# Seams of a two-layer hybrid block: the second statistic from sums of x*z, DMAs that accumulate into x, and a new order of VectorE's work

## The chip, the cores and the metric

One core of one Trainium2 chip runs the whole program. The metric is the device time in microseconds of one execution. In the texts PE is TensorE, DVE is VectorE, ACT is ScalarE, POOL is GpSimd and SP is SyncE. Lower is better.

## The reference

Two layers over 512 latent tokens and 256 context tokens (768 together, width 1024). Every sub-layer has the same frame, and the change is about that frame:

```python
def _pre(x, g, mod, k):
    return _rmsnorm(x, g) * (1.0 + mod[:, 3 * k + 1][:, None]) + mod[:, 3 * k][:, None]

def _post(x, y, g, mod, k, weight):
    return x + weight * mod[:, 3 * k + 2][:, None] * _rmsnorm(y, g)
# _rmsnorm: y = xf * rsqrt(mean(xf * xf) + EPS), times g
# per layer: x = _post(x, swiglu(_pre(x, .., 0)), ..); x = _post(x, mixer(_pre(x, .., 1)), ..)
#            x = _post(x, swiglu(_pre(x, .., 2)), ..)      the mixer: S5 heads beside 2-D Fourier heads
```

So between two sub-layers stand two root-mean-square statistics per token: that of the output y, and that of the new x.

## The kernel before, in words

Activations lie with the 1024 features in 8 chunks (KC) of 128 partitions and the 768 tokens along the free axis; the context takes columns 0 to 255. xT is the residual stream, yT the output of a stage. Weights come in units of 128x1024 values: SP loads one to `raw` (3 slots), ScalarE makes a rounded high part wH (L458), VectorE the rest wL (L465), and each product is three matmuls: high by high, high by low, low by high (L473). The activations are split in the same way into hH and hL. The counters w_hi, w_lo and w_used order this; `late` names a stage's one unit whose split waits for the end of the stage before: the third unit of the next stage.

The plan has six stages: f10, m0, f20 (layer 0: feed-forward, mixer, feed-forward), then f11, m1, f21 (layer 1; f21 has only the latent tokens, and so has the seam before it). Between two stages lies a seam. In the kernel before it goes like this.

- `last_chunks` (TensorE) makes the eight output chunks of a stage in three PSUM slots; `last_adds` (VectorE, L992, L1006, L1010) adds them to yT; ScalarE squares yT (L1384, L1398, L1401), GpSimd adds the squares of chunks 0 to 5 up in sumY (L1265), and TensorE sums over features with a matmul against ones (L1302), 32 columns to a block, so that VectorE can flip a row of sums into columns (L1310).
- ScalarE's root, VectorE's reciprocal (L1462), and a matmul with the identity (L1317) spread 1/rms over all partitions in PSUM.
- VectorE scales the eight chunks of y by it and by coefP, called P (L1471); the scaled output is weight*gate*norm(y). GpSimd adds chunks 0 to 3 into xT and VectorE chunks 4 to 7 (both L1282). VectorE then makes the low part of the late unit.
- ScalarE squares the new x (L1411), TensorE sums, and flip, root, reciprocal (L1487) and spread follow a second time.
- `pre_vector`: per chunk VectorE scales x into tmpN (L1496), ScalarE adds the shift and rounds to hH (L1423), VectorE makes hL (L1500). TensorE's `first_groups` takes the chunks as they come, with 2 units (mixer, f10) or 3 (feed-forward) held in PSUM at once, the last three chunks unit by unit.
- `keep_clock` (L1326) is filler on TensorE: products of the identity that nobody reads. `head_weights` makes products for the Fourier heads, copied to CW by ScalarE at the start of the mixer.

In the f1 stages and the mixers x is spilled to memory and its space reused; GpSimd reloads it before the end. In a mixer, `mix_tensor` goes on with projections (`proj`), between which it makes the inputs of the S5 states for a quarter of the heads (`state_inputs`); VectorE then turns, scans (L2105, L2106) and turns back each quarter. The first scan stands behind the low part of unit 7 in VectorE's order, and so behind projection 4. Each engine runs its instructions in the written order; semaphores are the only order between engines.

## Time and profile before

| | us |
|---|---|
| median of 3 runs | 2648.77 (2648.14 to 2652.62) |
| the profiled execution | 2646.27 |
| its span | 2644.5 |
| PE busy | 2586.2 (98%) |
| DVE busy | 1596.0 (60%) |
| POOL busy | 816.1 (31%) |
| ACT busy | 714.7 (27%) |

The span is the time between the first and the last instruction of the profile; outside it lie 1.8 us. A busy PE is not a useful PE: at the seams it runs sums and filler. Times in the rows below count from the start of the span.

### The profile page before, as it was taken

The numbers are of one execution on the slowest core, as the hardware profiler recorded it, in microseconds if no ns is written. First come the engines' busy times: TensorE is split into PE (matmuls) and PEld (weight loads), VectorE is DVE, ScalarE is ACT, GpSimd is POOL, SyncE is SP. The second block draws the span as 40 slices with busy tenths as digits, with TensorE's granted clock in tenths as the row PEclk, the third lists the DMA queues.
The fourth block names the chain that finished last, engine by engine and source line by source line (L and its number), as shares of the span: only waits on it lengthen the run. The fifth ranks groups of instructions, "written<-read, shape, count | busy, mean of one in ns | idle before, by whom it ended". The sixth has DMA issues, their size and how long they took to land.

```text
span 2644.5 us, 40750 instructions
## 1 busy us (share of the span) xinstructions
PE 2586.2 (98%) x17044; PEld 2429.9 (92%) x17044; DVE 1596.0 (60%) x2238; ACT 714.7 (27%) x1050; POOL 816.1 (31%) x1286
## 2 busy tenths in 40 slices
PE   6999999999999999999999999999999999999998
PEld 5999999998989899999999899999999878888886
DVE  6688878766574676676676633433343684544443
ACT  4222212123334411212113412122122424322223
POOL 1278876832140100000001148667651131000001
PEclk9999999999999999999999999999999999999999
DMA  9534444453364234434432422222223565233331
GB/s 338 154 123 156 157 143 133 161 187 132 117 194 144 79 98 136 130 108 138 136 104 91 109 67 83 94 92 90 94 88 116 189 196 163 72 96 96 96 96 64
DMA packets 346831, 334.54 MB, mean 127 GB/s; under 512 B 52496, under 2 KB 319896, under 8 KB 343576
## 3 DMA queue, kind: packets, MB, share of 16 engines
q1 hardware_dynamic: 284344, 198.19, 25.7%
q10 hardware_dynamic: 52288, 77.20, 8.7%
q0 software_dynamic: 10016, 56.56, 5.6%
q8 instruction: 134, 2.20, 0.3%
q14 instruction: 49, 0.40, 0.0%
HBM read 287.40 MB, written 44.50 MB: 126 GB/s over the span
## 4 chain that ended last, share of the span: by engine, by line
PE 86%; DVE 8%; POOL 2%; issue 1%; ACT 1%; DMA 1%; SPq 0%; DVEq 0%; POOLq 0%; ACTq 0%
PE ps L473 81%; POOL xT L1282 1%; DVE tmpN L1496 1%; DVE hL L1500 1%; PE ps L1302 1%; PE ps L1317 1%; DVE zb L2105 1%; DVE zd L2106 1%; PE ps L1050 1%; ACT wH L458 1%; PE ps L1069 1%; DVE zc L2118 0%; PE ps L1326 0%; DVE SR L2122 0%; PE ps L1702 0%
## 5 line engine op out<-in xcount | busy, mean ns | idle before, releaser
L473 PE MATMUL ps<-hH,wH 128*128 128x384 f32 (+1 forms) x2928 | 1013.5, 346 | 8.5 <-DVE hL L1500 8.0
L473 PE MATMUL ps<-hH,wL 128*128 128x384 f32 (+1 forms) x2928 | 1004.9, 343 | 0.0
L473 PE MATMUL ps<-hL,wH 128*128 128x384 f32 (+1 forms) x2928 | 1004.5, 343 | 0.0
L465 DVE TENSOR_TENSOR wL<-raw,wH 128x1024 fp32r<-128x1024 f32 x300 | 396.4, 1332 | 493.2 <-ACT wH L458 491.7
L473 PEld LDWEIGHTS ps<-hH,wH 128*128 128x128 f32 x2928 | 549.9, 188 | 35.4 <-DVE hL L1500 7.4
L473 PEld LDWEIGHTS ps<-hH,wL 128*128 128x128 f32 x2928 | 550.1, 188 | 18.1
L473 PEld LDWEIGHTS ps<-hL,wH 128*128 128x128 f32 x2928 | 550.2, 188 | 17.8
L473 PE MATMUL ps<-midH,wH 128*128 128x384 f32 (+1 forms) x1232 | 424.0, 344 | 2.9 <-DVE yT L948 2.5
L473 PE MATMUL ps<-midH,wL 128*128 128x384 f32 (+1 forms) x1232 | 421.5, 342 | 0.0
L473 PE MATMUL ps<-midL,wH 128*128 128x384 f32 (+1 forms) x1232 | 421.3, 342 | 0.0
L458 ACT ACTIVATE wH<-raw 128x1024 fp32r<-128x1024 f32 x300 | 310.9, 1049 | 366.2 <-PE ps L473 349.5
L1265 POOL TENSOR_TENSOR sumY<-sq 128x768 f32<-128x768 f32 (+1 forms) x6 | 10.0, 1659 | 1039.7 <-ACT sq L1384 1039.7
L584 DVE SCALAR_TENSOR_TENSOR adaW<-adaW,siluC 128x384 f32<-128x384 f32 x520 | 329.0, 684 | 0.8
L926 DVE TENSOR_TENSOR midF<-ps,sgate 128x768 f32<-128x768 f32 (+1 forms) x88 | 78.4, 890 | 318.1 <-PE ps L473 317.9
L948 DVE TENSOR_TENSOR yT<-ps,yT 128x768 f32<-128x768 f32 (+1 forms) x256 | 223.2, 885 | 71.3 <-PE ps L473 71.3
L473 PEld LDWEIGHTS ps<-midH,wH 128*128 128x128 f32 x1232 | 231.3, 188 | 13.4 <-DVE yT L948 5.3
L473 PEld LDWEIGHTS ps<-midL,wH 128*128 128x128 f32 x1232 | 231.4, 188 | 6.8
L473 PEld LDWEIGHTS ps<-midH,wL 128*128 128x128 f32 x1232 | 231.3, 188 | 6.8
L882 ACT ACTIVATE midH<-midF 128x768 fp32r<-128x768 f32 (+1 forms) x88 | 69.8, 793 | 575.0 <-DVE midF L926 575.0
L875 ACT ACTIVATE sgate<-ps 128x768 f32<-128x768 f32 (+1 forms) x88 | 66.9, 760 | 216.7 <-PE ps L473 206.1
L930 DVE TENSOR_TENSOR midL<-midF,midH 128x768 fp32r<-128x768 f32 (+1 forms) x88 | 81.8, 930 | 0.0
L666 ACT ACTIVATE modraw<-ps 128x3 f32<-128x3 f32 x76 | 9.1, 172 | 240.7 <-PE ps L473 240.7
(284 smaller groups left out, 2261.3 us busy)
## 6 DMA issues: line engine op xcount, KB each, us to landing
raw<-in_ffn_gu_dram SPq DMA_DIRECT2D x176, 512.0 KB, 3.9
adaW<-in_w_ada_dram ACTq DMA_DIRECT2D x40, 1536.0 KB, 7.0
raw<-in_ffn_down_dram SPq DMA_DIRECT2D x88, 512.0 KB, 3.5
x_d<-xT POOLq DMA_DIRECT2D x4, 3072.0 KB, 11.2
xT<-x_d POOLq DMA_DIRECT2D x4, 3072.0 KB, 10.6
ada_early<-in_w_ada_dram POOLq DMA_DIRECT2D x6, 1536.0 KB, 18.7
W_d<-gW POOLq DMA_DIRECT2D x16, 512.0 KB, 3.8
VT_d<-gVT ACTq DMA_DIRECT2D x16, 512.0 KB, 3.0
```

Source lines behind the costliest of these rows:

```text
L458: nc.scalar.activation(wH[:, n % SPLIT_SLOTS, :], raw[:, n % RAW_SLOTS, :], ACT.Copy).then_inc(w_hi, 1)
L465: nc.vector.tensor_tensor(wL[:, n % SPLIT_SLOTS, :], raw[:, n % RAW_SLOTS, :], wH[:, n % SPLIT_SLOTS, :].bitcast(f32), ALU.subtract).then_ ...
L473: ins = nc.tensor.matmul(dst, a, b, start=first and n == 0, stop=last and n == 3 * len(pairs) - 1)
L584: ins = stt(at, w[:, k], siluC[:, k, v:v + 1], adaP[:] if i == 3 else at, ALU.mult, ALU.add)
L875: nc.scalar.activation(sb_pair(sgate[:, f % 2, :], F.tok0), ps_pair(tile_slot(F, g), F.tok0), ACT.Silu)\
L882: nc.scalar.activation(midH[:, f % 4, F.tok0:TOK], midF[:, f % 2, F.tok0:TOK], ACT.Copy).then_inc(mid_hi, 1)
L926: nc.vector.tensor_tensor(sb_pair(midF[:, f % 2, :], F.tok0), ps_pair(tile_slot(F, g), F.tok0), sb_pair(sgate[:, f % 2, :], F.tok0), ALU.m ...
L930: nc.vector.tensor_tensor(midL[:, f % 4, F.tok0:TOK], midF[:, f % 2, F.tok0:TOK], midH[:, f % 4, F.tok0:TOK].bitcast(f32), ALU.subtract).t ...
L948: ins = nc.vector.tensor_tensor(sb_pair(yT[:, m, :], F.tok0), ps_pair(tile_slot(F, g + m), F.tok0), sb_pair(yT[:, m, :], F.tok0), ALU.add)
L1050: ins = nc.tensor.transpose(ps[:, 6 + a, t * 128:(t + 1) * 128], gV[:, a, t, :], ident[:])
L1069: ins = nc.tensor.matmul(ps[32 * p:32 * p + 32, 6 + g2, c0:c1], Bw[half, a, dd, p, :], rhs(half, a, dd, p), start=first, stop=last)
L1282: engine.tensor_tensor(xT[:, m, N.tok0:TOK], xT[:, m, N.tok0:TOK], yT[:, m, N.tok0:TOK], ALU.add)\
```

## The change

For each chunk, as it comes in the tail of a stage, VectorE also makes x*P*y (`cross_z`, P the factor that y will be scaled by but for 1/rms; z is P*y/rms(y)) and adds up those of chunks 0 to 5. TensorE sums the squares of y with weights of 1 and of P^2 at once (statP, columns 1 and 2) in bank 7, five chunks between the last chunks of the stage, and sums the cross products in bank 6 behind the stage. The sum of squares of the new x then is the old one (sumX is kept) plus 2*sum(x*P*y)/rms(y) plus sum(P^2*y^2)/rms(y)^2, made by VectorE in `new_sums` on six columns. GpSimd no longer adds squares or chunks of x: it makes the low part of the late unit (`late_lo`) and issues, for chunks 1 to 7, a DMA each that accumulates yT into xT; VectorE adds chunk 0. The row of 1/rms(y) is copied from PSUM to SBUF (rowY). VectorE scales y two chunks ahead (three in the latent seam) of making hL, within one loop (`joined_chunk`). `first_groups` waits for each unit by itself, interleaves all eight chunks, and holds three units in the mixer too, so the projections between which the state inputs stand begin at 3. Some of the mixer's loads move behind the fourth and eighth chunk. x has to be back before the tail instead of before its scaling. The last stage's end keeps the old way.

```diff
-    def first_groups(pe, base, count, pre, between=None):
-
-        pe.wait_ge(w_lo, base + count)
-        lead = KC - 3
+    def first_groups(pe, base, count, pre, between=None, cw_ready=None):
+
+        lead = KC if pre.after else KC - 3
         order = [(k, u) for k in range(lead) for u in range(count)]
         order += [(k, u) for u in range(count) for k in range(lead, KC)]
         for k, u in order:
             if u == 0:
                 pe.wait_ge(h_lo, KC * pre.nth + k + 1)
+            if k == 0:
+                pe.wait_ge(w_lo, base + u + 1)
+                if u == 1 and cw_ready:
+                    pe.wait_ge(cw, cw_ready)
+                if u == 2:
+                    pe.wait_ge(row_y, pre.after.nth + 1)
...
+    def cross_sums(pe, S, m):
+
+        pe.wait_ge(cross_x, cross_count(S, m))
+        return row_sums(pe, 6, crossed(S, m), S.tok0, TOK, m == 0, m == KC - 1)
+
+    def square_sums(pe, S, m, t0, t1, first=False, last=False):
+
+        return row_sums(pe, 7, sq[:, m, :], t0, t1, first, last, statP[:, m, :])
...
+            while S.next and m >= 2 and summed < m:
+                pe.wait_ge(sq_y, KC * S.post.nth + summed + 1)
+                square_sums(pe, S, summed, S.tok0, TOK, summed == 0)
+                summed += 1
...
+            wait_back(dve, S.post)
+            dlink(dve, nc.vector.memset(statP[:], 1.0))
+            dsync(dve)
+            dlink(dve, nc.vector.tensor_tensor(statP[:, :, 1:3], coefP[:], coefP[:], ALU.mult))
...
+            if S.next:
+                dve.wait_ge(S.read, S.read0 + m + 1)
+                ins = cross_z(dve, S, m, token_segments(S.tok0))
+                if 0 < m < CROSS_SUMMED:
+                    dlink(dve, ins)
+                    dsync(dve)
+                    ins = nc.vector.tensor_tensor(crossed(S, 0)[:, S.tok0:TOK], crossed(S, 0)[:, S.tok0:TOK],
+                                                  crossed(S, m)[:, S.tok0:TOK], ALU.add)
+                if m < CROSS_SUMMED - 1:
+                    dlink(dve, ins)
+                else:
+                    ins.then_inc(cross_x, 1)
...
+    def late_lo(pool, n):
+
+        if n >= NU:
+            return
+        pool.wait_ge(w_hi, n + 1)
+        nc.gpsimd.tensor_tensor(wL[:, n % SPLIT_SLOTS, :], raw[:, n % RAW_SLOTS, :],
+                                wH[:, n % SPLIT_SLOTS, :].bitcast(f32), ALU.subtract).then_inc(w_lo, 1)
+
+    def post_pool(pool, N, S):
+        for n in S.late:
+            late_lo(pool, n)
         wait_back(pool, N)
-        for m in POOL_CHUNKS:
...
+        for m in range(1, KC):
             pool.wait_ge(y_norm, KC * N.nth + m + 1)
-            add_to_x(pool, nc.gpsimd, N, m, x_new_pool)
-
-    def row_sums(pe, bank, squares, t0, t1, first, last):
+            pool.dma_start(xT[:, m, N.tok0:TOK], yT[:, m, N.tok0:TOK], accum_op=ALU.add).then_inc(x_added[m - 1], 16)
...
+    def post_tensor(pe, N, S):
+        if S.next is None:
+            end_sums(pe, N, S)
+            return
+        nxt = S.next
+        pe.wait_ge(sq_y, KC * N.nth + KC - 2)
+        square_sums(pe, S, KC - 3, N.tok0, TOK)
+        if N.tok0 == 0:
+            for m in (KC - 2, KC - 1):
+                pe.wait_ge(sq_half, 2 * N.nth + m - (KC - 2) + 1)
+                square_sums(pe, S, m, 0, HALF)
+        for m in (KC - 2, KC - 1):
+            pe.wait_ge(sq_y, KC * N.nth + m + 1)
+            ins = square_sums(pe, S, m, N.tok0 or HALF, TOK, False, m == KC - 1)
+        ins.then_inc(ss_y, 1)
+        for m in (0, KC - 2, KC - 1):
+            ins = cross_sums(pe, S, m)
+        ins.then_inc(ss_x, 1)
+        pe.wait_ge(rs_y, N.nth + 1)
+        spread_matmuls(pe, 4, 5, N.tok0, rstd, bc_y, bc_y_ctx)
+        keep_clock(pe, 2)
+        pre_spread(pe, nxt)
         if S.tag.startswith("f1"):
             head_weights(pe, S.gen)
-        else:
-            keep_clock(pe, 10)
-        wait_x(pe, N, 0)
         keep_clock(pe, 3)
+        pe.wait_ge(h_tmp, KC * nxt.nth + 1)
+        keep_clock(pe, 2)
+        pe.wait_ge(h_hi, KC * nxt.nth + 1)
...
+    def cross_z(dve, S, m, segments):
+
+        for t0, t1, v in segments:
+            ins = nc.vector.scalar_tensor_tensor(crossed(S, m)[:, t0:t1], yT[:, m, t0:t1], coefP[:, m, v:v + 1],
+                                                 xT[:, m, t0:t1], ALU.mult, ALU.mult)
+        return ins
...
+        if S.next:
+            root(act, rstdX[:], sumX[:], N.tok0, sum_x, N.nth + 1, sd_x)
+            act.wait_ge(y_norm, KC * N.nth + 1)
+            for t0, t1, v in token_segments(N.tok0):
+                ins = nc.scalar.activation(rowY[:, t0:t1], seg_ps(4, 5, v), ACT.Copy)
+            ins.then_inc(row_y, 1)
...
+    def scale_part(N, m, t0, t1, v, row):
+        return nc.vector.scalar_tensor_tensor(yT[:, m, t0:t1], yT[:, m, t0:t1], coefP[:, m, v:v + 1], row,
+                                              ALU.mult, ALU.mult)
+
+    def scale_y(dve, N, m):
+        for t0, t1, v in token_segments(N.tok0):
+            ins = scale_part(N, m, t0, t1, v, rowY[:, t0:t1] if N.has_next else seg_ps(2, 3, v))
+        ins.then_inc(y_norm, 1)
+
+    def add_part(t0, t1):
+        return nc.vector.tensor_tensor(xT[:, 0, t0:t1], xT[:, 0, t0:t1], yT[:, 0, t0:t1], ALU.add)
+
+    def new_sums(dve, N, S):
+
+        b = N.tok0 // 128
+        r, d, c, x = (t[:, b:6] for t in (rstd, sumD, cross, sumX))
+        dve.wait_ge(rs_y, N.nth + 1)
+        for b0, b1, v in [(b, 2, CTXV), (2, 6, LAT)][b // 2:]:
+            dlink(dve, nc.vector.tensor_tensor(sumD[:, b0:b1], turnedY[:, b0:b1, 1 + v], rstd[:, b0:b1], ALU.mult))
+        dsync(dve)
+        dlink(dve, nc.vector.tensor_tensor(d, d, r, ALU.mult))
+        dsync(dve)
+        dlink(dve, nc.vector.tensor_tensor(x, x, d, ALU.add))
+        dve.wait_ge(ss_x, N.nth + 2)
+        columns(dve, 6, N.tok0, cross).then_inc(cols_x, 1)
+        dve.wait_ge(cols_x, N.nth + 2)
+        dsync(dve)
+        dlink(dve, nc.vector.scalar_tensor_tensor(d, c, 2.0, r, ALU.mult, ALU.mult))
+        dsync(dve)
+        dlink(dve, nc.vector.tensor_tensor(x, x, d, ALU.add))
+        dsync(dve)
+        nc.vector.tensor_scalar(x, x, 0.0, None, ALU.max).then_inc(sum_x, 1)
+
     def post_vector(dve, N, S):
         dve.wait_ge(ss_y, N.nth + 1)
-        columns(dve, 2 * last_slot(S, 5), N.tok0, rstd).then_inc(cols_y, 1)
         b = N.tok0 // 128
+        if S.next:
+            nc.vector.transpose(turnedY[:, b:6].rearrange("p b i -> p (b i)"), ps[:, 7, 32 * b:192]).then_inc(cols_y, 1)
+        else:
+            columns(dve, 2 * last_slot(S, 5), N.tok0, rstd).then_inc(cols_y, 1)
         dve.wait_ge(sd_y, N.nth + 1)
         nc.vector.reciprocal(rstd[:, b:6], rstd[:, b:6]).then_inc(rs_y, 1)
-        if N.tok0 == 0:
-            dve.wait_ge(bc_y_ctx, N.ctx_nth + 1)
-        wait_back(dve, N)
-        dsync(dve)
-        for m in range(KC):
-            for t0, t1, v in token_segments(N.tok0):
-                if m == 0 and v == LAT:
-                    dve.wait_ge(bc_y, N.nth + 1)
-                ins = nc.vector.scalar_tensor_tensor(yT[:, m, t0:t1], yT[:, m, t0:t1], coefP[:, m, v:v + 1],
-                                                     seg_ps(2, 3, v), ALU.mult, ALU.mult)
-            ins.then_inc(y_norm, 1)
-        for m in DVE_CHUNKS:
-            dve.wait_ge(y_norm, KC * N.nth + m + 1)
-            add_to_x(dve, nc.vector, N, m, x_new)
-        for n in S.late[:1]:
-            split_lo(dve, n)
+        if S.next:
+            new_sums(dve, N, S)
...
+    def joined_chunk(dve, post, N, m, ahead):
+
+        dve.wait_ge(h_lo, KC * N.nth + m - 1 if m >= 2 else KC * N.nth + 1)
+        wait_x(dve, post, m)
+        for t0, t1, v in token_segments(N.tok0):
+            ins = scaled(N, m, t0, t1, v)
+        ins.then_inc(h_tmp, 1)
+        if m + ahead < KC:
+            scale_y(dve, post, m + ahead)
+        rest(dve, N, m)
+
+    def joined_vector(dve, post, N):
+
+        c, l = token_segments(0)
+        dve.wait_ge(bc_y_ctx, post.ctx_nth + 1)
+        dsync(dve)
+        dlink(dve, scale_part(post, 0, *c, seg_ps(4, 5, CTXV)))
+        inverse_x(dve, N)
+        dve.wait_ge(bc_y, post.nth + 1)
+        scale_part(post, 0, *l, seg_ps(4, 5, LAT)).then_inc(y_norm, 1)
+        dsync(dve)
+        dlink(dve, add_part(*c[:2]))
+        dve.wait_ge(y_norm, KC * post.nth + 1)
+        add_part(*l[:2]).then_inc(x_new, 1)
+        dve.wait_ge(bc_x_ctx, N.nth + 1)
+        dsync(dve)
+        scaled(N, 0, *c).then_inc(h_tmp_ctx, 1)
+        dve.wait_ge(row_y, post.nth + 1)
+        scale_y(dve, post, 1)
+        dve.wait_ge(bc_x, N.nth + 1)
+        wait_x(dve, post, 0)
+        scaled(N, 0, *l).then_inc(h_tmp, 1)
+        scale_y(dve, post, 2)
+        dve.wait_ge(h_hi_ctx, N.nth + 1)
+        low(0, *c)
+        dve.wait_ge(h_hi, KC * N.nth + 1)
+        low(0, *l).then_inc(h_lo, 1)
+        for m in range(1, KC):
+            joined_chunk(dve, post, N, m, 2)
...
+        load_units(RAW_SLOTS, 5)
+        sp.wait_ge(h_lo, KC * pre.nth + 5)
         load_states(0)
         load_states(1)
         load_phases(0)
-        load_units(RAW_SLOTS, 5)
         sp.wait_ge(h_lo, KC * pre.nth + KC)
         load_phases(1)
+        load_units(5, 7)
         load_chunks(0)
         load_chunks(1)
-        load_units(5, 7)
         sp.wait_ge(b_ps, M.n0["b_ps"] + 1)
         load_states(2)
         load_chunks(2)
...
-        first_groups(pe, M.base, 2, pre)
+        first_groups(pe, M.base, 3, pre, None, M.gen.n0["cw"] + 1)
...
-        for m in range(2, 8):
+        for m in range(3, 8):
             proj(m)
-            if m >= 2 and m < 6:
-                state_inputs(m - 2)
+            if m < 7:
+                state_inputs(m - 3)
...
-                    square_x(act, nxt, lambda m: wait_x(act, N, m))
-                    root(act, rstdX, nxt.tok0, nxt.nth, cols_x, sd_x)
-                    add_shift(act, nxt)
+                    add_shift(act, nxt, 0, 1)
+                    if S.tag.startswith("f1"):
+                        take_head_weights(act, S.gen)
+                    add_shift(act, nxt, 1, KC)
...
-                    flip_rows(dve, nxt)
-                    inverse_x(dve, nxt)
-                    for n in S.late[1:]:
-                        split_lo(dve, n)
-                    pre_vector(dve, nxt)
+                    (joined_vector_latent if nxt.tok0 else joined_vector)(dve, N, nxt)
```

## Rows read from the trace of the kernel before

**Rows 1.** The page: the chain that ended last, share of the span by engine.

```profile
PE 86%; DVE 8%; POOL 2%; issue 1%; ACT 1%; DMA 1%; SPq 0%; DVEq 0%; POOLq 0%; ACTq 0%
```

**Rows 2.** Chain of waits, seam f20 to f11: start us, us, what held it.

```profile
1455.65 0.57 DVE yT L1010
...
1460.72 7.17 POOL xT L1282 x4
...
1473.03 0.40 DVE rstdX L1310
...
1478.11 21.93 PE ps L473 x125
```

**Rows 3.** Timeline of ScalarE: start us, duration; in brackets idle before, releaser.

```profile
1457.88 1.04 ACT L458 ACTIVATE wH<-raw 128x1024 fp32r<-128x1024 f32 x1
...
1503.36 0.82 ACT L875 ACTIVATE sgate<-ps 128x768 f32<-128x768 f32 x1 [0.33 <-PE ps L473]
...
2274.83 0.60 ACT L875 ACTIVATE sgate<-ps 128x512 f32<-128x512 f32 x1 [2.64 <-PE ps L473]
```

**Rows 4.** Chain of waits, the latent seam m1 to f21.

```profile
2243.26 0.70 DVE yT L992
...
2262.26 37.91 PE ps L473 x166
```

**Rows 5.** Chain of waits, the two mixers: end of stage before, first scan.

```profile
635.18 0.57 DVE yT L1010
...
711.59 0.35 DVE zb L2105
...
2045.49 0.57 DVE yT L1010
...
2118.68 0.35 DVE zb L2105
```

**Rows 6.** Timeline of VectorE, tail of f20 and the seam behind it.

```profile
1426.82 0.17 DVE L1441 TENSOR_TENSOR coefP<-modraw,adaB 128x16 f32<-128x16 f32 x1
1427.02 0.17 DVE L1443 SCALAR_TENSOR_TENSOR coefP<-coefP,gT 128x16 f32<-128x16 f32 x1
...
1439.01 0.96 DVE L992 TENSOR_TENSOR yT<-ps,yT 128x768 f32<-128x768 f32 x1 [2.85 <-PE ps L473]
...
1447.32 0.96 DVE L992 TENSOR_TENSOR yT<-ps,yT 128x768 f32<-128x768 f32 x1 [2.54 <-PE ps L473]
...
1458.01 0.19 DVE L1462 RECIPROCAL rstd<-rstd 128x6 f32<-128x6 f32 x1 [0.37 <-ACT rstd L1376]
1459.00 0.48 DVE L1471 SCALAR_TENSOR_TENSOR yT<-yT,coefP,ps 128x256 f32<-128x256 f32 x1 [0.80 <-PE ps L1317]
...
1471.39 1.22 DVE L465 TENSOR_TENSOR wL<-raw,wH 128x1024 fp32r<-128x1024 f32 x1
...
1475.67 0.75 DVE L1496 SCALAR_TENSOR_TENSOR tmpN<-xT,coefA,ps 128x512 f32<-128x512 f32 x1 [0.41 <-PE ps L1317]
```

**Rows 7.** Timeline of TensorE in that seam: a group of sums, then filler.

```profile
1470.67 0.53 PE L1302 MATMUL ps<-sq,ones 128*32 128x192 f32 x8
1471.13 0.49 PE L1326 MATMUL ps<-ident 128*128 128x128 f32 x2
```

**Rows 8.** Timelines of GpSimd and VectorE, tail of m0: the two at once.

```profile
869.83 1.85 POOL L1265 TENSOR_TENSOR sumY<-sumY,sq 128x768 f32<-128x768 f32 x1 [1.65 <-ACT sq L1384]
870.67 2.09 DVE L465 TENSOR_TENSOR wL<-raw,wH 128x1024 fp32r<-128x1024 f32 x1 [1.86 <-ACT wH L458]
```

**Rows 9.** DMA issues by line: KB each, median us from issue to landing.

```profile
E_d<-EG POOLq DMA_DIRECT2D x2, 384.0 KB, 3.1
...
x_d<-xT POOLq DMA_DIRECT2D x1, 3072.0 KB, 11.2
raw<-in_w_in_dram SPq DMA_DIRECT2D x4, 512.0 KB, 7.3
```

**Rows 10.** Busy time by stretch, middle of m1; PEclk is the granted clock.

```profile
2144.00:2147.00 3.00, 1.93 (x3) 0.87 (x4) 2.93 (x4) 0.00 (x0) 0.00 (x0) 0.78 1.04 352
```

More of the change, by code:

```diff
@@ L267, in build @@
     x_new = sem("x_new")
-    x_new_pool = sem("x_new_pool")
+    x_last = sem("x_last")
+    x_added = [sem(f"x_added{m}") for m in range(1, KC)]
     sq_x = sem("sq_x")
@@ L416, in build @@
         p[1].next = p[3]
+        p[2].has_next = p[3] is not None
         pre.after = N
@@ L1477, in post_vector @@
-        for n in S.late[:1]:
-            split_lo(dve, n)
+        if S.next:
+            new_sums(dve, N, S)
+        else:
+            wait_back(dve, N)
+            dve.wait_ge(bc_y, N.nth + 1)
+            dsync(dve)
+            for m in range(KC):
+                scale_y(dve, N, m)
+            for m in range(LAST_POOL, KC):
+                dve.wait_ge(y_norm, KC * N.nth + m + 1)
+                add_to_x(dve, nc.vector, N, m, x_last)
     def flip_rows(dve, N):
         dve.wait_ge(ss_x, N.nth + 1)
-        columns(dve, N.banks[0], N.tok0, rstdX).then_inc(cols_x, 1)
+        columns(dve, N.banks[0], N.tok0, sumX).then_inc(cols_x, 1)
@@ new lines, in scaled, with low, rest @@
+    def scaled(N, m, t0, t1, v):
+        return nc.vector.scalar_tensor_tensor(tmpN[:, m % 2, t0:t1], xT[:, m, t0:t1], coefA[:, m, v:v + 1],
+                                              seg_ps(*N.banks, v), ALU.mult, ALU.mult)
+    def low(m, t0, t1, v):
+        return nc.vector.scalar_tensor_tensor(hL[:, m, t0:t1], tmpN[:, m % 2, t0:t1], coefS[:, m, v:v + 1],
+                                              hH[:, m, t0:t1].bitcast(f32), ALU.add, ALU.subtract)
+    def rest(dve, N, m):
+        dve.wait_ge(h_hi, KC * N.nth + m + 1)
+        for t0, t1, v in token_segments(N.tok0):
+            ins = low(m, t0, t1, v)
+        ins.then_inc(h_lo, 1)
@@ new lines, in joined_vector_latent @@
+    def joined_vector_latent(dve, post, N):
+        l = token_segments(N.tok0)[0]
+        inverse_x(dve, N)
+        dve.wait_ge(bc_y, post.nth + 1)
+        dsync(dve)
+        scale_part(post, 0, *l, seg_ps(4, 5, LAT)).then_inc(y_norm, 1)
+        dve.wait_ge(y_norm, KC * post.nth + 1)
+        add_part(*l[:2]).then_inc(x_new, 1)
+        dve.wait_ge(row_y, post.nth + 1)
+        scale_y(dve, post, 1)
+        dve.wait_ge(bc_x, N.nth + 1)
+        wait_x(dve, post, 0)
+        scaled(N, 0, *l).then_inc(h_tmp, 1)
+        scale_y(dve, post, 2)
+        rest(dve, N, 0)
+        scale_y(dve, post, 3)
+        for m in range(1, KC):
+            joined_chunk(dve, post, N, m, 3)
@@ L1934, in mix_scalar @@
             proj(m)
[L1935 to L1936 removed]
+            if m >= 3 and m < 7:
+                take_inputs(m - 3)
             if m == 5:
```

175 lines of the change are left out of this document (92 added, 83 removed).

## The prediction

> **What bounds the kernel now.** I read the page first (busy shares, chain), then the chain of waits around each stage end, then the timelines of VectorE, ScalarE and TensorE there, the DMA table, and the windows for the granted clock. TensorE is busy 98% of the span (page, part 1) and holds 86% of the chain [rows 1], so time is won only where it does filler or waits. That is at the seams, between the last matmul of a stage and the first matmuls of the next. Call the start of VectorE's last addition T. In the seam before the second layer [rows 2] T is 1455.65. GpSimd's four additions to x take 7.17 us, squares and sums of the new x follow, its statistic is flipped at 1473.03 (T+17.4), and the first real matmul comes at 1478.11 (T+22.4). From there TensorE is dense: the third unit's group is done when ScalarE's second gate starts at 1503.36 [rows 3], T+47.7, so a chunk of three units costs 25.2/8 = 3.16 us. Four seams have this form (two into a feed-forward half, two into a mixer). The fifth, latent tokens only, goes from 2243.26 to 2262.26 [rows 4]; unit 0 of its three is done at 2274.83 [rows 3] after 18 of 24 unit-chunks, so 0.70 each, 2.1 a chunk, and all end at 2279.1 (T+35.8). After a mixer's seam the next limit is VectorE's scan, first issued T+76.4 in layer 0 and T+73.2 in layer 1 [rows 5].
>
> **The change part by part.**
>
> *The second statistic.* It leaves the chain that waits for x: 7.17 us of GpSimd, eight squares and their sums. In their place stands new_sums. Its start is the old one: the reciprocal is at 1458.01 and ends T+2.55 [rows 6]. Three cross sums of x*z now stand ahead of the first spread on TensorE, at 0.46 us each (from one group's start to the next instruction's, 1470.67 to 1471.13 [rows 7]): they end T+3.05, against a reciprocal at T+2.55, so +0.45. VectorE's dependent small operations cost 0.20 us each from start to start (the two coefP rows of [rows 6]), and a flip 0.40 [rows 2]: four small ones, the flip, three small ones give the sum at T+4.3.
>
> *GpSimd takes the third unit's low part.* It may start when ScalarE's high part is done, 1457.88+1.04 = T+3.3 [rows 3]. GpSimd takes 1.85 us for 768 columns [rows 8], so 2.45 for 1024: until T+5.75. They also show that the two engines don't share: VectorE's split, started at 870.67 while GpSimd's addition runs to 871.68, ends at 872.76, 1.08 after GpSimd and 2.09 long, against 1.22 alone [rows 6]. The last two steps of new_sums (c times r, the addition) read two SBUF tiles from T+3.6 on and would stand until T+5.75. Bounds 0 (six-column operations slip through) and 2.1 us; I take 2.0, as the row is of the same two kinds of instruction. Sum at T+6.3. It saves VectorE 1.22 us, which was beside TensorE's filler.
>
> The Trainium skill, "SBUF — State Buffer", section "Who interferes with whom", says that a VectorE instruction with two SBUF inputs is locked out by a GpSimd one that reads SBUF until that finishes. By it the stall is the full 2.1 us, without it nothing; the durations of [rows 8] agree with it for 1024 columns, and no row shows it for six.
>
> *First chunk.* Root 0.31, reciprocal 0.2, scale 0.75, two additions 1.05, context scale 0.45, chunk 1's scale 1.1, latent scale 0.7, chunk 2's scale 1.1, low parts 1.15 (durations as L1471, L1496 and L1500 in rows 6, 0.48 for 256 and 0.75 for 512 columns, less where back to back): h_lo of chunk 0 at T+13.5, 8.9 before the old one.
>
> *DMAs accumulate into x.* No row shows one. Nearest are GpSimd's queue with 384 KB in 3.1 us and 3072 KB in 11.2 [rows 9]. An accumulation has to read x beside y, 768 KB in for 384 written; on the line between the rows that is 4.3 us from the normalized y to x usable. Bounds: 3.1 (reading costs nothing) and 11.2 (as the large one); 7.3, the loads of [rows 9] under contention, lies between. I take 4.3, nearest to the row of equal size. A joined chunk costs VectorE 1.14+1.1+1.12 = 3.35 us where it still scales y (chunks 1 to 5), 2.25 after. Chunk 1's x comes at 10.5+4.3 = T+14.8, a stall of 1.3; later ones were scaled two chunks before, which leaves 2x3.35-2.3 = 4.4 us and just covers 4.3. h_lo of chunk 7 comes at T+37, TensorE ends its 3.16 us chunks at T+41.1. Above 4.4 the pitch is (2.3+L)/2.
>
> The Trainium skill, "Collectives: The Full Stack", section "Stop ④ — SDMA + CCE: where bytes move and the add happens", holds that the add itself is free and that the cost is the second read, which doubles the read side; its measured ratio is 1.93. That would put the pure moving time of 384 KB at twice that of a copy, near my line; no row here shows either.
>
> *All eight chunks interleaved.* The three units now finish within the last chunk instead of 6.3 us apart, so unit 3's split is uncovered: unit 0 is done 2.1 before the end, gate and high part take 0.77+1.05, the low part 1.22: TensorE waits 1.0 us. In a mixer the store copies come first, about 2.3.
>
> *Tail.* Five groups of square sums move in front of T, 0.46 each: +2.3 us of TensorE per full seam (latent 0.35: +1.75). VectorE's cross products cost 1.14 a chunk and 0.96 for adding them up, with the addition (0.96) 3.1, with a split every second chunk 7.5 for two; TensorE's two chunks take 8.3 (y's additions at 1439.01 and, two chunks on, at 1447.32 [rows 6]) and 0.9 for the new sums, so they are covered, with 1.7 us left in two chunks. I book 0.15 at T.
>
> *Mixer order.* Three projections before the first state inputs, which come one projection later; the scan's gate is the low part of unit 7, after projection 4. With groups done at T+41.1, stall 2.3, projection 8.4, inputs 2.8, late chunk loads 0.8, projection 8.5, copies and high part 1.6, low part 1.2: scan at T+67.1 against 76.4 (layer 1: 64.1 against 73.2). Loads of states moved behind chunk 4 leave the queue to the accumulations; they are wanted 20 us later. Spilling x starts some 20 us later and the scans need it only at T+55.
>
> **The sum.** Feed-forward seams: 47.9-(41.1+1.0)-2.3 = 3.6, twice 7.2. Mixers: 76.4-67.1-2.3 = 7.0 and 73.2-64.1-2.3 = 6.8. Latent, with the same steps at 512 columns: first chunk T+11.5, end T+30.8; 35.8-31.8-1.75 = 2.2. Together 23 us. The profiled execution took 2646.3 (span 2644.5); the median is 2648.8, 0.1% more. 2648.8-23 = 2626.
>
> **The rivals.**
> *No lock-out.* If six-column operations pass GpSimd's, each seam starts 2.0 us earlier: 10 more, 33 in all, 2616. For it: nothing in the trace shows a small one standing. Against: [rows 8].
> *Accumulations slower than their cover, the slower side.* One mechanism: the pitch follows (2.3+L)/2 once L passes 4.4. At 5.8 us the gain is 2; that is the point of no change. At 6.5 the feed-forward seams lose 4.0 each, mixers 0.7, latent 2.3: 12 slower, 2661; at 7.3, as the loads of [rows 9], 27 slower, 2676; at 11.2, 101. For it: each accumulation is read, read, write, issued by a queue the trace knows only for plain copies, and in the mixers spills and loads crowd in. Against: at the seams before feed-forward halves the DMA queues are nearly empty.
> *It turns out fast.* L 3.1: 29 faster with the stall, 39 without: 2610.
> *The clock.* TensorE now has 1.9 us of waiting twice, with little filler between T+5 and T+13.5. In the middle of a mixer TensorE idles for a DMA (busy 1.93 of 3 us [rows 10]) and the granted clock is 0.78, a mix of the levels 2.4 and 1.2 GHz. Here chunk 0 at half rate costs 3.2 us, of which TensorE's wait for chunk 1 absorbs half, and the spreads 1.6: at most 3 us a seam, 15 in all, 2641. It alone does not turn the sign.
>
> **How the numbers follow.** Stall and L near 4.3: 0.42, 2626, its own range 2616 to 2636. No lock-out or quick accumulations: 0.25, 2608 to 2618. Clock or a smaller loss that eats part: 0.10, 2636 to 2645. Slow accumulations: 0.23, from 2646 on; a sixth of these falls within no change. A measurement of this kernel can't tell less than 0.2% (5.3 us) from nothing. So faster 0.76, same 0.05, slower 0.19. The range leaves out a tenth at either end: 2608 to 2656.
>
> **What would show it.** Right: x's flip some 3.5 us after T instead of 17.4; first seam matmul near T+13.5; VectorE's joined chunks 3.35 us apart with a stall at chunk 1 alone; an accumulation landing in about 4; one small VectorE operation of some 2 us beside GpSimd's split; 1 to 2 us before unit 3; scans at T+67. Wrong: pitches over 4 us with VectorE waiting for the DMA; TensorE's tail chunks spaced more than 4.7 apart (VectorE late with the cross products); a granted clock under 1 at the seams.

## The result, and the profile after

The changed kernel took 2671.33 us (median of 4 runs, 2662.73 to 2672.87), the kernel before 2648.45 beside it: ratio 1.0071, 95% interval 1.0051 to 1.0092. That is 19 us slower by the ratio (22.9 by the medians, 24.2 between the two profiled executions), where 23 us faster was forecast. The profiled execution took 2670.47 us, span 2668.7, at a mean granted clock of 0.988 (before 0.998).

Its page: the busy shares, and the chain by engine, which answers to [rows 1].

```profile
span 2668.7 us, 40329 instructions
PE 2571.4 (96%) x16764; PEld 2413.7 (90%) x16764; DVE 1649.8 (62%) x2371; ACT 687.6 (26%) x1019; POOL 779.8 (29%) x1281
...
PE 85%; DVE 7%; DMA 3%; issue 2%; ACT 2%; SPq 0%; POOL 0%; ACTq 0%; DVEq 0%; POOLq 0%
```

TensorE's share fell by two points, and DMA is now on the chain. Cutting both executions at T, the start of VectorE's last addition of each stage, tells where (lengths in us; the forecast has the tail's cost in the stage that ends with it):

| stretch | before | after | difference | forecast |
|---|---|---|---|---|
| start to T of the first half | 635.18 | 639.13 | +3.95 | +2.3 |
| mixer 0 | 240.99 | 246.91 | +5.9 | -7.0 |
| second half, layer 0 | 579.48 | 581.70 | +2.2 | -3.6 |
| first half, layer 1 | 589.84 | 588.75 | -1.1 | -3.6 |
| mixer 1 | 197.77 | 213.63 | +15.9 | -7.4 |
| last half (latent seam) | 378.84 | 375.87 | -3.0 | -4.0 |

The mixers hold 36 of the 47 us by which these differences miss the forecast. Of the 36, 27 lie between T and the first scan, 9 behind it. Now VectorE's timeline in the seam into mixer 0 (columns: start, duration, engine, line, operation, tiles, count, and in brackets the idle time before it and what ended it); T is 639.13. It answers to [rows 2, 6]. (Numbers in brackets behind hL, h_lo or "chunk" count from 0, so chunk 7 is the last.)

```profile
642.28 0.38 DVE L1390 TRANSPOSE_TENSOR_REDUCE cross<-ps 128x6 f32<-128x192 f32 x1
642.69 2.17 DVE L1607 SCALAR_TENSOR_TENSOR sumD<-cross,rstd 128x6 f32<-128x6 f32 x1
644.89 0.17 DVE L1609 TENSOR_TENSOR sumX<-sumX,sumD 128x6 f32<-128x6 f32 x1
...
650.46 1.14 DVE L1650 SCALAR_TENSOR_TENSOR hL<-tmpN,coefS,hH 128x256 fp32r<-128x256 f32 x2
653.52 1.14 DVE L1646 SCALAR_TENSOR_TENSOR tmpN<-xT,coefA,ps 128x256 f32<-128x256 f32 x2 [1.91 <-DMA xT<-yT]
...
671.19 1.14 DVE L1646 SCALAR_TENSOR_TENSOR tmpN<-xT,coefA,ps 128x256 f32<-128x256 f32 x2 [0.63 <-DMA xT<-yT]
673.52 1.15 DVE L1650 SCALAR_TENSOR_TENSOR hL<-tmpN,coefS,hH 128x256 fp32r<-128x256 f32 x2 [1.19 <-ACT hH L1546]
679.35 1.14 DVE L1646 SCALAR_TENSOR_TENSOR tmpN<-xT,coefA,ps 128x256 f32<-128x256 f32 x2 [4.68 <-DMA xT<-yT]
```

The head of the seam goes as forecast. A multiplication of six columns stands 2.17 us beside GpSimd's low part, h_lo of chunk 0 comes at T+12.5, and the first wait for an accumulation is 1.91 us. The end does not: chunk 7's accumulation, issued at 669.57, is ready at 679.26, 9.7 us later, and h_lo(7) comes at T+43.7 (T+46.0 in mixer 1; T+37.8 before). The DMA issues of that stretch, 664 to 683 us (columns: line, queue, count, KB each, median us to landing):

```profile
x_d<-xT POOLq DMA_DIRECT2D x1, 3072.0 KB, 10.7
VTs<-VT_d SPq DMA_DIRECT2D x2, 1024.0 KB, 8.5
Es<-E_d SPq DMA_DIRECT2D x2, 768.0 KB, 10.8
xT<-yT POOLq DMA_DIRECT2D x2, 384.0 KB, 7.3
```

What it does to TensorE is in the windows of 4 us (columns: busy time and count of each engine, granted clock, busy share of the DMA engines, GB/s). First the changed kernel, T+36 to T+48 and T+56 to T+64:

```profile
675.10:679.10 4.00, 3.02 (x18) 2.70 (x16) 0.00 (x0) 0.00 (x0) 0.00 (x0) 1.00 1.04 334
679.10:683.10 4.00, 0.22 (x1) 0.22 (x2) 2.29 (x4) 1.12 (x2) 0.57 (x1) 0.95 0.86 358
683.10:687.10 4.00, 4.00 (x16) 4.00 (x17) 0.00 (x0) 1.54 (x2) 0.00 (x0) 0.62 1.02 395
...
695.10:699.10 4.00, 3.26 (x19) 2.94 (x17) 0.76 (x1) 2.45 (x4) 0.00 (x0) 1.00 1.10 315
699.10:703.10 4.00, 1.37 (x33) 1.40 (x35) 2.06 (x20) 1.86 (x3) 0.00 (x0) 1.00 0.71 210
```

Then the kernel before, T+16 to T+32:

```profile
651.20:655.20 4.00, 3.81 (x38) 2.88 (x37) 2.00 (x4) 1.36 (x3) 0.57 (x1) 1.00 0.69 287
655.20:659.20 4.00, 3.83 (x27) 3.52 (x26) 3.99 (x7) 1.87 (x4) 0.00 (x0) 1.00 1.06 455
659.20:663.20 4.00, 3.45 (x19) 2.94 (x18) 3.79 (x9) 2.28 (x5) 0.00 (x0) 1.00 0.12 49
663.20:667.20 4.00, 4.00 (x24) 3.67 (x22) 3.96 (x8) 2.15 (x4) 0.00 (x0) 1.00 0.00 0
```

Before, the spill of x (3 MB) ran at T+16 and the state loads near T, and from T+28 to T+36 the DMA engines stood still. Now the state loads start at T+28 and the spill at T+41, and the engines are busy 0.7 to 1.1 of the time until T+64. In that time unit 0's output (UP) must go out to u_d in memory and come back in another layout (UC) before the first state inputs. The stores, before (676 to 690 us) and after (684 to 700):

```profile
u_d<-UP ACTq DMA_DIRECT2D x3, 384.0 KB, 3.3
```

```profile
u_d<-UP ACTq DMA_DIRECT2D x4, 384.0 KB, 6.1
```

In the same stretches the loads of units 5 and 6 take 11.8 us instead of 7.0 (medians). The scans start at T+78.0 and T+80.3, against T+76.4 and T+73.2 in [rows 5]. TensorE's waits, summed from 620 us to the end, tell where it stands. Behind them, for comparison, are those of the runs that the next section describes:

| kernel | waits for hL | waits at the state inputs | ratio |
|---|---|---|---|
| before | 3.8 | 0 | 1 |
| changed | 26.0 | 5.1 | 1.0071 |
| e1, state loads back | 13.9 | 20.6 | 1.0064 |
| e12, and unit loads back | 14.4 | 13.1 | 1.0054 |
| e5, and low part on VectorE | 15.0 | 12.0 | 1.0027 |
| a0, changed kernel with only the traffic spread | 11.8 | 0 | 0.9998 |
| t1, kernel before with the late traffic | 3.8 | 20.2 | 1.0082 |

So in the changed kernel itself most of what the traffic costs stands at chunk 7's accumulation, and only 5.1 us at the state inputs. Against a0 the two sums differ by 19 us, as the times do.

The clock needs its own measure. Over all 4 us windows, TensorE's busy time multiplied by the missing share of the clock is 25.2 us, against 3.8 before. The low windows lie right behind waits of TensorE. Two are behind the wait for chunk 1 (904 and 2076 us), two behind the wait for the second statistic ahead of chunk 0 (1472 and 2276), one behind unit 3's stall (932). In the seam into mixer 0 the clock stays at 1.00 until chunk 7. The rest are in the mixers and at both ends of the kernel. The 3.8 us are those of a good execution: the profiled one of the kernel before has a mean clock of 0.998, and the median of the 11 to 25 executions beside each set of runs has 0.995 to 0.996. Among those executions each thousandth of clock goes with 2.7 to 3.0 us of time, about what the product gives (2.6 us); which of the two drives the other isn't shown.

### The profile page after: what moved, and what is told of

Read it like the earlier page. It is cut to its first block, busy times and chain, and to the rows that moved or that the text cites. A ratio compares the mean times of both kernels' runs of the same rounds, so it can differ in the third digit from the quotient of the medians.

```text
span 2668.7 us, 40329 instructions
## 1 busy us (share of the span) xinstructions
PE 2571.4 (96%) x16764; PEld 2413.7 (90%) x16764; DVE 1649.8 (62%) x2371; ACT 687.6 (26%) x1019; POOL 779.8 (29%) x1281
## 4 chain that ended last, share of the span: by engine, by line
PE 85%; DVE 7%; DMA 3%; issue 2%; ACT 2%; SPq 0%; POOL 0%; ACTq 0%; DVEq 0%; POOLq 0%
PE ps L484 79%; DMA xT<-yT 2%; DVE tmpN L1646 1%; PE ps L1985 1%; DVE yT L1581 1%; DVE hL L1650 1%; ACT wH L469 1%; ACT hH L1546 1%; PE ps L1381 1%; PE ps L1957 1%; PE ps L1912 1%; PE ps L1108 1%; PE ps L1127 1%; DMA xin<-in_x_dram 0%; PE ps L640 0%
## 5 line engine op out<-in xcount | busy, mean ns | idle before, releaser
L476 DVE TENSOR_TENSOR wL<-raw,wH 128x1024 fp32r<-128x1024 f32 x295 | 379.0, 1296 | 450.3 <-ACT wH L469 448.4
L484 PEld LDWEIGHTS ps<-hL,wH 128*128 128x128 f32 x2928 | 554.0, 189 | 17.8
L961 DVE TENSOR_TENSOR midF<-ps,sgate 128x768 f32<-128x768 f32 (+1 forms) x88 | 78.4, 890 | 314.2 <-PE ps L484 314.1
L1359 POOL TENSOR_TENSOR wL<-raw,wH 128x1024 fp32r<-128x1024 f32 x5 | 11.7, 2339 | 807.8 <-ACT wH L469 807.8
```

The lines of the kernel that those rows point to most:

```text
L476: nc.vector.tensor_tensor(wL[:, n % SPLIT_SLOTS, :], raw[:, n % RAW_SLOTS, :], wH[:, n % SPLIT_SLOTS, :].bitcast(f32), ALU.subtract).then_ ...
L484: ins = nc.tensor.matmul(dst, a, b, start=first and n == 0, stop=last and n == 3 * len(pairs) - 1)
L961: nc.vector.tensor_tensor(sb_pair(midF[:, f % 2, :], F.tok0), ps_pair(tile_slot(F, g), F.tok0), sb_pair(sgate[:, f % 2, :], F.tok0), ALU.m ...
```

## The experiments

Theory A: the mixers' transfers, moved behind the last chunks, sit in the way of the chain that feeds the state inputs. Theory B: the loss is the granted clock behind TensorE's new waits. Theory C: the tail's sum groups. Theory D: the lock-out, VectorE's small operation standing until GpSimd's low part is done. Ratios are to the kernel before, with 95% intervals; 0.1% is 2.65 us.

### Undoing parts of the change

**State loads back (e1).**
```diff
-        sp.wait_ge(h_lo, KC * pre.nth + 5)
+        sp.wait_ge(h_lo, KC * pre.nth + 7)
         load_states(0)
```


> Only the wait ahead of the mixers' state and phase loads goes back: they are issued after chunk 7's h_lo, as in the kernel before, not after chunk 5's. Theory A (the last chunk's accumulation queues behind 2.75 MB of state loads): chunk 7's accumulation in m0 falls from 9.7 to about 4.5 us, in m1 from 11.2 to about 4.5, h_lo(7) comes at T+38 to 39 in both (from T+43.7 and T+46.0), and each scan some 5 us earlier, unless the loads, issued about 10 us later, are then what a unit waits for; whole kernel 2671 less 5 to 11, 2660 to 2666. Theory B (the loss is the granted clock in the mixers): the accumulation may shorten, but the scans come no more than 2 us earlier and the time stays above 2668.


Seven chunks' h_lo are now waited for instead of five. Measured 1.0064 (1.0050 to 1.0079). h_lo(7) came at T+38.7 and T+39.6, as theory A had it, but the scans at T+81.8 and T+81.8: later. The loads had left the accumulations' way and entered the state inputs'. (My label "as in the kernel before" was not right: there these loads go out near T.)

**And the unit loads behind the chunk loads (e12).**
```diff
-        load_units(5, 7)
         load_chunks(0)
         load_chunks(1)
+        load_units(5, 7)
```


> As e1_loads_back, and SP issues the loads of weight units 5 and 6 behind the chunk loads again, as before. Theory A: TensorE's 3.4 us wait for the UC loads in m0 and the 5 us wait for in_w_in in m1 go too; the scans come at about T+68 to 70 in both mixers (from T+78.0 and T+80.3), the time is 2650 to 2658. Theory B (clock): the waits go, the idle they leave is less, but the span of stages behind stays as in the changed kernel; over 2663.


1.0054 (1.0041 to 1.0068), scans at T+78.4 and T+78.8. A gain of some 3 us over the last, not the 10 to 20 expected.

**The low part on VectorE (e3).**
```diff
-        for n in S.late:
-            late_lo(pool, n)
...
         low(0, *l).then_inc(h_lo, 1)
+        split_lo(dve, S.late[0])
```


> Only the late unit's low part goes back to VectorE, right behind chunk 0's h_lo, where VectorE otherwise waits 1.9 us for chunk 1's accumulation; GpSimd has only the issues. Theory D (lock-out is a cost on the path): new_sums loses its 2.0 us stall, h_lo(0) at T+10.5 instead of T+12.5 in full seams, the low part fills most of the stall at chunk 1, five seams times 1.5 to 2 us: 2661 to 2664. If the stall at chunk 1 is not free for it (accumulations also come 2 us earlier), the saving is under 0.8 us a seam: 2667 or more.


1.0028 (1.0018 to 1.0038): 11 us less. The two rows that answer to the stalled pair above, of this kernel:

```profile
642.14 0.17 DVE L1605 SCALAR_TENSOR_TENSOR sumD<-cross,rstd 128x6 f32<-128x6 f32 x1
642.34 0.17 DVE L1607 TENSOR_TENSOR sumX<-sumX,sumD 128x6 f32<-128x6 f32 x1
```

0.17 us in place of 2.17, and h_lo(0) at T+10.5 in all four full seams: theory D holds, at 2.0 us a seam.

**All three (e5).**


> State loads behind chunk 7's h_lo, unit loads behind the chunk loads, the low part on VectorE; the statistic from sums and the accumulating transfers stay. Theory A plus D: 2641 to 2650, so no slower than the kernel before; scans at T+66 to 69. Theory B (clock) or C (the tail's sum groups and the accumulations are dearer than the old seam even without these three): 2655 or more.


1.0027 (1.0016 to 1.0038), no better than the low part alone, and slower than the 2641 to 2650 us expected. h_lo(7) was early (T+36.6), yet TensorE waited 12.0 us in two waits for UC:

```profile
PE ps L1912 <- DMA UC<-u_d: 12.0, 2, 6.1
```

That turned theory A from "accumulations queue behind loads" into A2: spill, state loads and the round trip of u_d share one crowded stretch, and whatever is moved within it only trades waits.

**Work in TensorE's waits (f1, theory B).** Of the last two units the chunk-0 products are made twice, 12 matmuls in the 2.0 us wait for chunk 1, and 20 small matmuls run ahead of the wait for the first state inputs:
```diff
+        if pre.after:
+            order[count:count] = [(0, u) for u in range(count - 2, count)]
...
+            if q == 0:
+                pe.wait_ge(proj_read, M.n0["proj_read"] + 3)
+                for _ in range(20):
+                    nc.tensor.matmul(ps[:, 1, 0:128], ident[:], ident[:], start=True, stop=True)
```


> The changed kernel with work that keeps TensorE busy where it waits: at each full or latent seam the chunk-0 groups of the last two units are computed twice (12 matmuls, about 2.0 us, the length of the wait for chunk 1), and in the mixers 20 small matmuls run ahead of the wait for the state inputs. Nothing else moves. Theory B (the clock): the rows of 4 us in which the granted clock falls to 0.5 to 0.8 right behind each seam's chunk-1 wait go; these rows hold about 25 us of busy time times missing clock over the kernel, against 4 in the kernel before, of which some 7 to 10 us lie behind the chunk-1 waits: 2661 to 2665. Theory A (transfers in the mixers alone): the time stays within 2 us of 2671, or rises by up to 3 us where the repeated matmuls outlast the wait.


1.0079 (1.0064 to 1.0095): no gain, and the product of busy time and missing clock was still 23.0 us, since the clock fell elsewhere (0.57 ahead of the first matmuls, 0.5 behind Tz). It refutes neither: it hardly moved what it was to move.

**Without the five sum groups in the tail (e4, theory C).** Both statistics then count only the squares of chunks 5 to 7, so part of the computation is left out.
```diff
-            while S.next and m >= 2 and summed < m:
+            while False:
```


> The changed kernel without five of the eight square-sum groups between the last output groups of each stage (only chunks 5 to 7 are counted in the second statistic, so part of the computation is left out). Theory C: the five groups cost 0.63 us each on the path, 3.1 us a full seam and less in the latent one, five stages: 2671 less 13 to 16, 2655 to 2658. If VectorE, with its cross products between, sets the end of the tail and not TensorE: under 5 us less.


1.0030 (1.0017 to 1.0044), 11 us less, somewhat short of the 13 to 16. VectorE's first addition of the last eight starts 26.38 us ahead of T in the kernel before (in the seam into layer 1), 29.39 in the changed kernel, 26.31 here: the groups cost 3.0 us a full seam by this spacing. The whole kernel's 11 us are what the forecast had booked for five seams (four of 2.3 and one of 1.75), so the two measures differ.

### Spreading the transfers

In e6 the spill goes out by chunks as accumulations land, and the state loads go out near T as before; low part and unit loads as in "All three".
```diff
+    def spill_chunk(pool, m):
+        pool.dma_start(x_d[:, m * TOK:(m + 1) * TOK], xT[:, m, :]).then_inc(x_spill, 16)
...
+            if N.spill_next and m >= 2:
+                wait_x(pool, N, m - 2)
+                spill_chunk(pool, m - 2)
...
         load_states(0)
         load_states(1)
         load_phases(0)
         load_units(RAW_SLOTS, 5)
-        sp.wait_ge(h_lo, KC * pre.nth + 7)
```


> e5 (low part on VectorE, unit loads behind the chunk loads) with the DMA traffic of the mixers taken out of the time behind the last accumulations: the state and phase loads (2.75 MB) go back ahead of the seam, and the 3 MB spill of x goes out chunk by chunk as each accumulation lands, not in one piece behind the last. Theory A2 (UP to u_d to UC is the chain that sets the first state inputs, and 5.9 MB of spill and state loads lie in its way): TensorE's wait of 5.9 us at the first state inputs of m0 and its like in m1 go, scans at T+65 to 69 (from T+76.8 and T+77.9 in e5), the time 2659 less 14 to 20: 2639 to 2645, below the kernel before. Theory B alone (clock): the waits shrink but the time stays within 5 us of 2659. If spilling beside the accumulations lengthens these from 4.0 to over 5 us, each of the three seams with a spill gives back 5 us or more.


0.9976 (0.9965 to 0.9986): faster than the kernel before, 13.5 us below "All three" and just short of the 14 to 20 expected. The UC waits are gone, u_d lands in 3.3 us again, scans at T+71.4 and T+69.5. Its product of busy time and missing clock is 22.5 us, against 27.8 in "All three", so some 5 of the 13.5 us may be the clock and the rest is not.

Each half alone, first the spill (e6a), then the loads (e6b):


> e5 with only the spill of x going out chunk by chunk; the state loads stay behind chunk 7's h_lo. Theory A2 with both loads in the way in proportion to their bytes (3.1 of 5.9 MB): about half of the 14 us that e6 gained on e5, 2650 to 2654.


0.9974 (0.9962 to 0.9985).


> e5 with only the state and phase loads ahead of the seam; the spill stays in one piece behind the last accumulation. By bytes the other half, 2650 to 2654; if the loads next to the first accumulations delay h_lo(1), less is gained: 2655 or more.


0.9982 (0.9972 to 0.9991). Not half the gain each, but nearly all: with either 3 MB out of the stretch the rest nearly fits. The terms don't add; I read it as an overflow. In the profiles of the two some 6 to 7 us of waits at the state inputs are left, against 0.8 with both, and the scans come up to 4 us later.

**The same traffic in the old kernel (t1).** No part of the new seam, only the changed kernel's order of the spill and the loads:
```diff
+            pool.wait_ge(h_lo, KC * pre.nth + KC)
...
+        load_units(RAW_SLOTS, 5)
+        sp.wait_ge(h_lo, KC * pre.nth + 5)
         load_states(0)
...
-        load_units(RAW_SLOTS, 5)
...
+        load_units(5, 7)
         load_chunks(0)
         load_chunks(1)
-        load_units(5, 7)
```


> The kernel before with nothing of the new seam, only the changed kernel's order of transfers: the 3 MB spill of x waits for the last h_lo, the state and phase loads wait for chunk 5's h_lo and stand behind units 3 and 4, and units 5 and 6 stand ahead of the chunk loads. Theory A2 (traffic behind the last chunk sits in the chain UP, u_d, UC, state inputs): TensorE waits 3 to 8 us at the first state inputs of each mixer, the scans come 4 to 9 us later after T than 76.4 and 73.2, 8 to 18 us in all: 2658 to 2667. Theory B (clock alone, traffic hidden): within 3 us of the kernel before.


1.0082 (1.0066 to 1.0097), 22 us slower, beyond the upper end. Its u_d stores in mixer 0 (676 to 692 us), and then its waits of TensorE at the state inputs (total, times, longest):

```profile
u_d<-UP ACTq DMA_DIRECT2D x2, 384.0 KB, 12.7
```

```profile
PE ps L1704 <- issue: 20.2, 2, 10.5
```

A store of 384 KB takes 12.7 us instead of 3.3, and TensorE stands 20.2 us in two waits where it stood in none. Scans: T+88.4 and T+85.1.

**Traffic alone in the changed kernel (a0).** The spill and the state loads as in e6, the rest as changed.


> The changed kernel with only the transfers moved: state and phase loads ahead of the seam, the spill chunk by chunk; the low part stays on GpSimd, units 5 and 6 stay ahead of the chunk loads. If traffic and lock-out add up: 1.0071 less 13.5 us of 2650, about 1.002 of before. If the lock-out and the order of unit loads hide the gain: above 1.005. If the low part on GpSimd cost only through late transfers: below 0.999.


0.9998 (0.9989 to 1.0007): 19 us less than the changed kernel. The product of busy time and missing clock is 24.3 us, against 25.2, so these 19 us are not the clock. They are more than the 13.5 which the same two edits gave between "All three" and e6. With them in place the low part and the order of unit loads bring only another 6 (to 0.9976), where the low part brought 11 before.

### The clock

**The kernel before without its filler (c1).**


> The kernel before without its filler matmuls at the seams, so TensorE is idle where it waits there; no result depends on them. Theory B (idle at a seam drops the granted clock behind it): rows of 4 us at 0.5 to 0.8 appear behind each of the five seams, 15 to 25 us of busy time times missing clock in all against 4, and the kernel is 8 to 20 us slower. Theory A2 alone: no change in the clock rows, and a time within 2 us of before.


1.0043 (1.0028 to 1.0057). Windows of it, in the seam into mixer 0:

```profile
648.00:652.00 4.00, 3.58 (x36) 0.91 (x40) 4.00 (x5) 3.67 (x5) 0.49 (x1) 0.50 0.01 3
652.00:656.00 4.00, 2.94 (x18) 2.27 (x19) 1.15 (x4) 0.70 (x2) 0.08 (x1) 0.50 0.92 393
656.00:660.00 4.00, 1.53 (x9) 1.26 (x8) 3.21 (x6) 1.06 (x3) 0.00 (x0) 0.86 0.92 393
```

The clock is at the lower of its levels (1.2 GHz) for most of each of the five seams, and some 8 us of the product lie in the middle of mixer 1. The product rises from 3.8 to 44.9 us; the time by 11 by the ratio, by 20 between the two profiled executions. So idle at a seam does lower the clock and that costs, but a half to a quarter of the product. That TensorE is mostly waiting there anyway is the likely reason, not a tested one.

**Fillers on e6.** Repeated products as above (f6):


> e6 with the repeated chunk-0 groups at the seams. Theory B: another 5 to 8 us below e6, about 2633 to 2638. Theory A2 alone: no difference from e6, or up to 2 us above it.


0.9997 (0.9988 to 1.0005), 5.6 us slower than without, though its product fell to 17.8. In profiles the loss stands in mixer 1 (T to T 204.97 against 201.66), where h_lo(7) came 2.1 us later; what made it so I can't tell.

16 small matmuls ahead of each mixer's waits for the transform tables and for Tz (the inputs of its last products, loaded from memory). The second place (g1):
```diff
-            pe.wait_ge(set_c[q], M.n0["set_c"] + 16 * (1 + T8))
             if q == 0:
                 pe.wait_ge(pq, M.n0["pq"] + HC)
+                for _ in range(16):
+                    nc.tensor.matmul(ps[:, 4, 0:128], ident[:], ident[:], start=True, stop=True)
+            pe.wait_ge(set_c[q], M.n0["set_c"] + 16 * (1 + T8))
```


> e6 with 16 small filler matmuls (about 2.2 us) ahead of each mixer's wait for the transform tables and of its wait for the Tz and Ws loads, the two stretches behind which the granted clock fell to 0.5 for up to 12 us in the second mixer of e6 (5.1 us of busy time times missing clock between 2180 and 2262) and not in the kernel before. Theory B (a drop costs what the rows show): these rows go back to 1.00, D to E shortens by 4 to 5 us, the kernel from 0.9976 to about 0.996 of before. Rival (in these stretches TensorE is not what the time hangs on, or the drop comes anyway): within 2 us of e6.


0.9983 (0.9975 to 0.9991), as e6 within the intervals, where 0.996 was expected. But mixer 1 from scan to end took 127.1 us in place of 132.2. The windows behind the Tz wait, e6:

```profile
2178.10:2182.10 4.00, 2.25 (x22) 2.18 (x22) 2.18 (x4) 0.42 (x2) 0.00 (x0) 0.99 0.50 103
2182.10:2186.10 4.00, 4.00 (x42) 4.00 (x40) 0.00 (x0) 0.00 (x0) 0.00 (x0) 0.50 0.30 60
2186.10:2190.10 4.00, 4.00 (x30) 3.59 (x29) 0.00 (x0) 0.78 (x3) 0.00 (x0) 0.50 0.46 103
2190.10:2194.10 4.00, 4.00 (x15) 3.17 (x14) 0.69 (x1) 1.25 (x3) 0.00 (x0) 0.73 0.90 302
```

and with the fillers:

```profile
2180.60:2184.60 4.00, 4.00 (x31) 2.50 (x28) 0.21 (x1) 2.02 (x4) 0.00 (x0) 1.00 1.20 247
2184.60:2188.60 4.00, 4.00 (x41) 3.11 (x39) 4.00 (x5) 2.33 (x4) 0.00 (x0) 1.00 0.53 114
2188.60:2192.60 4.00, 4.00 (x54) 3.69 (x51) 0.08 (x1) 0.72 (x3) 0.00 (x0) 1.00 0.29 59
```

Mixer 0, which has one wait of 0.7 us to cover, paid for them instead: from T to T it took 244.6 us in place of 238.6. So, in mixer 1 alone (g2):
```diff
+                for _ in range(16 if tok0 else 0):
```


> e6 with the filler matmuls of g1 in the second mixer alone, where TensorE has waits of 2.3 and 2.7 us to cover; the first mixer has only one of 0.7 us, and g1 paid there for matmuls that cover nothing. Theory B as g1 left it (scan to the end of the second mixer fell from 132.2 to 127.1 us, the gain eaten in the first mixer): 4 to 6 us below e6, 0.9955 to 0.9965 of before. Rival (g1's shorter second mixer was chance): as e6, 0.997 to 0.999.


0.9963 (0.9949 to 0.9977), median 2640.73 us: 3.4 us below e6, just under the 4 to 6 expected; the intervals of the two overlap, so this sum by itself is not clear of noise. It is the fastest version, 10 us below the kernel before. Scan to end of mixer 1 is 127.4 us, again 5 less than e6, and mixer 0 takes 239.2.

## Why the prediction was wrong

**The step that failed** is in "Mixer order": "Loads of states moved behind chunk 4 leave the queue to the accumulations; they are wanted 20 us later. Spilling x starts some 20 us later and the scans need it only at T+55." I asked when each moved transfer is wanted and found slack for each. I did not ask what else moves in the stretch where they now run. There they hold back two things that someone waits for: chunk 7's accumulation, and the round trip of u_d, which the forecast booked as "late chunk loads 0.8" and which sets the first state inputs. Moving the loads off the one put them onto the other (e1). Priced both ways: taken out of the changed kernel, 19 us (12 to 27 by the ends of the intervals); put into the old one, 22 us (17 to 26). That is the whole of the loss against the kernel before, and less than half of the distance to the forecast: without it the change is worth nothing, not 23 us. In profiles the forecast put the scans at T+67.1 and T+64.1; they came 11 and 16 us later.

**Right.** The place of the second statistic, with h_lo(0) at T+12.5 (forecast 13.5, and T+22.3 before). The lock-out, 2.0 us a seam from a row of 768 columns: the operation took 2.17 us and 0.17 without it. The Trainium skill ("SBUF — State Buffer", "Who interferes with whom") names this lock-out; it stands here for six columns, and goes when GpSimd's low part goes. The accumulation: 4.3 us forecast, 4.0 measured (median of 28). The pitch of the joined chunks, 3.35 forecast, 3.39 measured. Unit 3's stall in the first half of layer 1: 1.0 forecast, 1.11 measured; and it started at T+43.4, against 42.1.

**The slow-accumulation rival** had the right sign and half the mechanism. I had written "in the mixers spills and loads crowd in", but let it act on every chunk through L; in the trace it acts on chunk 7 (9.7 and 11.2 us), and once that was cleared (e1), on transfers that the rival did not name.

**The tail** was mis-sized: 2.3 us a full seam booked, 3.0 measured by the spacing of additions, with e4's profile beside it. Five groups cost 0.6 each by it, not 0.46.

**The VectorE bound.** The forecast of h_lo(7) at T+37 was not far off where nothing crowds (T+38.8), but with the lock-out gone it still is T+36.7 to 38.1, and before it was T+37.8: the new seam gives TensorE its first chunk 10 us earlier and its last no earlier. VectorE's 3.39 us a chunk, against TensorE's 3.16, eats the lead. The forecast had 2.25 us for the last two chunks, where nothing is left to scale; they also came 3.39 apart, since VectorE waited 1.19 us for ScalarE's hH in each (the row at 673.52 above). What is left is some 4.5 us at the end of the groups, and the tail takes 3.0 back. That is why the two halves with a full seam lose 2.2 and gain 1.1, not 3.6 each. In layer 0 two more waits come on top: chunk 7's accumulation took 5.24 us and unit 3's stall was 2.0.

**The clock** was a rival at 0.10, "at most 3 us a seam, 15 in all". Its mechanism is there. The one place where it could be taken out by itself, behind mixer 1's Tz wait, gave 3.4 us of the whole, inside the noise, and 5 us of mixer 1 in two profiles. The seams' own share stays open: f1 and f6 moved it too little, and c1 shows that at the seams the product of busy time and missing clock overstates it, 2 to 3.6 times (41 us against 20 between the profiles, 11 by the ratio).

**The account.** From -23 to +19 are 42 us. Transfers 19; tail 0.7 in each of five stages, 3 to 4; the clock in mixer 1 about 3 of what e6 leaves. The rest, some 16, is measured as a whole (a0 is at 0, forecast -23) and not one by one: late h_lo(7), unit 3's stall in layer 0, the mixers' scans, 1 and 7 us late in a0 and 4 and 5 in e6, and the clock at the seams. That none of these is large was seen in traces; how they share it was not tested. Some written sums of the forecast also come out lower than what it entered: its steps give T+13.1 for 13.5 (first chunk), 36.1 for 37 (h_lo(7)), 66.7 for 67.1 (scan), and the old groups end at 47.7 in one place and 47.9 in another. All but the last made it the more cautious, so they aren't what went wrong.

## What to carry to other kernels

For each transfer that an edit moves, sum the bytes of everything that runs in its new place, and look for a round trip there whose landing someone waits for; that the moved transfer itself has slack proves nothing. Putting only the new order of transfers into the old kernel is one cheap run and gives the price at once. And where a start is won by 10 us, compute the last chunk too: the slower pitch decides what is left at the end. Filler pays only where there is a wait of its length.
